# Twelve matmuls of a unit in another order: each weight part right behind the same stationary operand

## What is computed

```python
mod = silu(c) @ w_ada + b_ada                       # shift, scale, gate_res
h = rms(x) * norm_w * (1 + scale) + shift           # (256, 4096)
q, k, v, z_a, f_logit, x_r, z_r = split(h @ w_in)   # 4096 -> 12304 columns
y_a = (forgetting_attention(rms(q), rms(k), v, f_logit) * silu(z_a)) @ w_br_attn
y_r = (rg_lru(causal_conv(x_r)) * silu(z_r)) @ w_br_rnn
g_a, g_r = split(sigmoid(h @ w_gate + b_gate))
y = x + gate_res * ((g_a * y_a + g_r * y_r) @ w_out)
```

## Time and profile before

| | |
|---|---|
| time, median of 3 runs | 2731.93 us (2727.08 to 2733.43) |
| span of the profiled execution, first to last instruction | 2723.2 us |
| median less that span | 8.7 us |
| busy PE, PEld, DVE, ACT | 95%, 78%, 71%, 45% of the span |
| matmuls and weight loads | 11618 and 11618 |
| DMA | 701.95 MB, mean 258 GB/s |

### The profile page before, as it was taken

One profiled execution on the slowest core, in us unless ns is written; L12 is line 12 of the kernel. 1 busy time (PEld: TensorE's weight loads), 2 busy tenths in 40 slices (PEclk: granted clock), 3 DMA queues, 4 the chain that ended last, 5 costly groups with the idle time before them and its releaser, 6 DMA issues.

```text
span 2723.2 us, 37753 instructions
## 1 busy us (share of the span) xinstructions
PE 2580.2 (95%) x11618; PEld 2131.3 (78%) x11618; DVE 1929.6 (71%) x2038; ACT 1227.1 (45%) x1437; POOL 1.2 (0%) x9
## 2 busy tenths in 40 slices
PE   0199999999999999999999999999999999999999
PEld 0178888888888788787888888887888888788887
DVE  6688988989884656565666666668888888745454
ACT  1044444444445544445555555554444444433333
POOL 0000000000000000000000000000000000000000
PEclk9999999999999999999999999999999999999999
DMA  8999999999985565444666666669999999766665
GB/s 314 302 359 328 359 337 329 363 332 350 347 287 162 179 194 163 133 147 148 200 197 196 197 196 196 197 198 343 324 328 331 331 330 332 252 206 220 213 224 169
DMA packets 370084, 701.95 MB, mean 258 GB/s; under 512 B 26482, under 2 KB 30804, under 8 KB 369748
## 3 DMA queue, kind: packets, MB, share of 16 engines
q1 hardware_dynamic: 370004, 700.93, 76.6%
HBM read 696.65 MB, written 4.19 MB: 257 GB/s over the span
## 4 chain that ended last, share of the span: by engine, by line
PE 92%; DMA 3%; issue 2%; DVE 2%; ACT 1%; SPq 0%; ACTq 0%; DVEq 0%
PE ps_acc L1130 29%; PE ps_acc L1132 29%; PE ps_acc L1137 29%; DMA ada_land<-in_w_ada 2%; DVE acc L673 1%; DMA land<-in_w_gate 1%; PE ps_t L1229 1%; PE ps_t L1228 1%; PE ps_t L1293 1%; PE ps_c L1158 1%; ACT w_hi L451 0%; PE ps_t L1149 0%; PE ps_t L1286 0%; PE ps_c L1299 0%; PE ps_t L1220 0%
## 5 line engine op out<-in xcount | busy, mean ns | idle before, releaser
L659 DVE TENSOR_TENSOR w_lo<-land,w_hi 128x1024 fp32r<-128x1024 f32 x896 | 1093.8, 1222 | 622.1 <-ACT w_hi L451 618.8
L451 ACT ACTIVATE w_hi<-land 128x1024 fp32r<-128x1024 f32 x896 | 950.5, 1061 | 1253.2 <-PE ps_acc L1132 1090.6
L1130 PE MATMUL ps_acc<-w_hi,h_hi 128*128 128x512 f32 x3072 | 1207.3, 393 | 5.7 <-ACT w_hi L451 5.7
L1132 PE MATMUL ps_acc<-w_hi,h_lo 128*128 128x512 f32 x3072 | 1197.7, 390 | 0.0
L1137 PE MATMUL ps_acc<-w_lo,h_hi 128*128 128x512 f32 x3072 | 821.9, 389 | 3.7 <-DVE w_lo L659 3.7
L1130 PEld LDWEIGHTS ps_acc<-w_hi,h_hi 128*128 128x128 f32 x3072 | 577.7, 188 | 125.7 <-ACT w_hi L451 6.9
L1137 PEld LDWEIGHTS ps_acc<-w_lo,h_hi 128*128 128x128 f32 x3072 | 576.6, 188 | 124.9 <-DVE w_lo L659 4.1
L1132 PEld LDWEIGHTS ps_acc<-w_hi,h_lo 128*128 128x128 f32 x3072 | 577.9, 188 | 118.7
L673 DVE SCALAR_TENSOR_TENSOR acc<-ada_land,cvec,acc 128x1024 f32<-128x1024 f32 x248 | 317.1, 1279 | 32.0 <-DMA ada_land<-in_w_ada 28.1
L1008 DVE SCALAR_TENSOR_TENSOR racc<-res_land,cvec,racc 128x512 f32<-128x512 f32 x248 | 185.7, 749 | 4.9
L1130 PE MATMUL ps_acc<-w_hi,yr_hi 128*128 128x512 f32 x256 | 103.2, 403 | 0.0
(11 more groups left out here) (166 smaller groups left out, 1084.2 us busy)
## 6 DMA issues: line engine op xcount, KB each, us to landing
land<-in_w_in SPq DMA_DIRECT2D x384, 512.0 KB, 4.7
ada_land<-in_w_ada SPq DMA_DIRECT2D x256, 512.0 KB, 5.5
land<-in_w_gate SPq DMA_DIRECT2D x256, 512.0 KB, 4.3
res_land<-in_w_ada SPq DMA_DIRECT2D x128, 512.0 KB, 7.6
land<-in_w_out SPq DMA_DIRECT2D x128, 512.0 KB, 3.5
land<-in_w_br_attn SPq DMA_DIRECT2D x64, 512.0 KB, 3.5
land<-in_w_br_rnn SPq DMA_DIRECT2D x64, 512.0 KB, 5.8
gate<-in_b_gate SPq DMA_DIRECT2D x32, 256.0 KB, 5.2
```

What stands on the lines that cost most here:

```text
L451: act.activation(w_hi[:, u % PARTS], land[:, u % LAND], ACT.Copy).then_inc(hi_rdy, 1)
L659: dve.tensor_tensor(w_lo[:, u % PARTS], land[:, u % LAND], w_hi[:, u % PARTS].bitcast(F32), ALU.subtract).then_inc(split_done, 1)
L1130: pe.matmul(out, left_hi(kk, t), w_hi[:, u % PARTS, kk], start=first and kk == 0, stop=False)
L1132: ins = pe.matmul(out, left_lo(kk, t), w_hi[:, u % PARTS, kk], start=False, stop=False)
```

## The change

The twelve matmuls of `unit` are issued in another order, with (kk, t) after each: low left by high weights 00, high left by high weights 00, the same two for 01, then, after the wait for `split_done`, high left by low weights 01; low and high left by high weights 10, high left by low weights 10; low and high left by high weights 11, high left by low weights 11; and last high left by low weights 00. Three of the four matmuls by low weights so follow a matmul with the same stationary operand. The wait for the low weights stands before the fifth matmul and not before the ninth. `hi_used` is raised by the tenth matmul and not by the eighth, and `unit_done` by the twelfth as before. Nothing is added or left out.

```diff
-                for kk in range(UK):
-                    for t in range(NT):
-                        out = ps_acc[:, par, t]
-                        pe.matmul(out, left_hi(kk, t), w_hi[:, u % PARTS, kk], start=first and kk == 0,
-                                  stop=False)
-                        ins = pe.matmul(out, left_lo(kk, t), w_hi[:, u % PARTS, kk], start=False, stop=False)
-                ins.then_inc(hi_used, 1)
+
+                def by_hi(kk, t):
+                    out, right = ps_acc[:, par, t], w_hi[:, u % PARTS, kk]
+                    pe.matmul(out, left_lo(kk, t), right, start=first and kk == 0, stop=False)
+                    return pe.matmul(out, left_hi(kk, t), right, start=False, stop=False)
+
+                def by_lo(kk, t, end):
+                    return pe.matmul(ps_acc[:, par, t], left_hi(kk, t), w_lo[:, u % PARTS, kk],
+                                     start=False, stop=last and end)
+
+                by_hi(0, 0)
+                by_hi(0, 1)
                 pe.wait_ge(split_done, n0 + u + 1 + LAND)
-                for kk in range(UK):
-                    for t in range(NT):
-                        ins = pe.matmul(ps_acc[:, par, t], left_hi(kk, t), w_lo[:, u % PARTS, kk],
-                                        start=False, stop=last and kk == UK - 1)
-                ins.then_inc(unit_done, 1)
+                by_lo(0, 1, False)
+                by_hi(1, 0)
+                by_lo(1, 0, False)
+                by_hi(1, 1).then_inc(hi_used, 1)
+                by_lo(1, 1, True)
+                by_lo(0, 0, True).then_inc(unit_done, 1)
```

## The result

| | before | changed |
|---|---|---|
| median, 15 runs each | 2731.11 us | 2735.71 us |
| range | 2723.17 to 2734.51 us | 2734.54 to 2737.10 us |
| span of the profiled execution | 2723.2 us | 2734.4 us |

The ratio is 1.0022, with a 95% interval of 1.0014 to 1.0030. The two spans differ by 11.2 us, as the sum said (11). The two medians differ by only 4.6 us. Before's runs fall in two groups, 7 of 15 at or under 2727.1 us and 8 at or over 2731.1, and the changed kernel's in one.

A forecast was written before the change was run, and what follows sets the result against it. PE, carrying 92% of the chain, was taken as the bound. Stalls of 1.4 + 4.2 + 1.5 + 1.8 + 1.0 + 0.5 + 0.6 = 11 us on 2731.93 us gave 2743 us; range 2725 to 2750 us.

The forecast's parts named there:

- the distance of two starts: Between matmuls in a unit: stays 0.227 us despite repeated stationary operands and the new bank order; effect taken as 0.
- the rival: In the units' matmuls: a repeated stationary operand shortens the distance, gaining 7 to 27 us against 11 us of stalls; chance 0.18.
- The shift: In steady units: the later `hi_used` makes ACT's copy and DVE's subtraction 0.45 us later, reserve falling from 1.96 to 1.5 us.
- The stalls: Where low weights come too little ahead of the fifth matmul, PE waits: 11 us in sum, 5 to 20 us.
- Recurrent blocks: Units like 451 and 439: new stalls of 4.2 us and 1.5 us.
- unit 451's kind: In the recurrent blocks, once per 24 units: reserve 0.09 us, so 0.53 us of stall, 8 times, 4.2 us.
- unit 439's kind: In the recurrent blocks: reserve 0.40 us, so 0.22 us of stall, 7 times, 1.5 us.
- swallowed shift: At the tight places: PE's other products release DVE and ACT, so only unit 279 pays; 2733 us, chance 0.15.
- Squares and half-wave starts: Units 248 to 276, every fourth, behind ACT's squares: 0.22 us, 8 times, 1.8 us; six earlier half-wave starts: 1 us.
- Unit 279: Behind DVE's chain: 1.4 us more wait; a longer low-clock stretch, 0 to 1.6 us, taken as 0.
- The second merge pass: Unit 583 and four behind it: 0.5 us; waits for DVE in the last merge job: 0.6 us.
- 8.7 us around it: Time outside the profiled span, added to the 2734.2 us span to give 2742.9 us.

The follow-up runs named there:

- wait5: The kernel before with only the wait for the low weights moved from before the ninth to before the fifth matmul; median 2727.73 us, ratio interval 0.9978 to 0.9996.
- before_again: The kernel before, run once more with no edit; median 2732.75 us, ratio 0.9996 to the kernel before.
- spread_after: The changed kernel with the forget gate's 17 DVE scan operations issued two at a time behind units 286 to 303; median 2728.88 us, ratio 0.9994.
- best_after: The changed kernel with the forget gate's scan in pieces and z_r's sigmoid and product moved from unit 17 to 30; 2724.4 us, ratio 0.9983.
- best_before: The kernel before with the forget gate's scan in pieces and z_r's sigmoid and product moved from unit 17 to 30; 2715.9 us, ratio 0.9952.

## Why the prediction was right, step by step

**The bound, and the distance of two starts.** Both held. The distance did not move with the stationary operand, nor with the order of the banks: units 600 to 751 are the same to 0.01 us in all orders. The size of the rival was mis-added, though: 2743 less 7 to 27 us is 2716 to 2736 us with 2726 in the middle, not 2739 and 2724. The small product's 0.11 against 0.12 us did not carry over; the argument for that, that the load is shorter than the distance here and as long as it there, fits, but no run varied the load alone. Also by this the Trainium skill's sentence ("TensorE: Matmul & The Clock Gate", Part 2) that one can load once and multiply repeatedly finds nothing to save here: all 11618 loads are made in every order.

**The shift.** ACT's copy for unit 450 stood at 1466.85, 4.21 us before its unit's start (1473.78 - 2.72 = 1471.06); after the change at 1473.76, 3.75 us before (1480.23 - 2.72 = 1477.51). So it came 0.46 us later, 0.45 forecast.

**The stalls.**
- Recurrent blocks: 4.35 us of 5.7 forecast. The 8 places of unit 451's kind hold all of it, 4.35 / 8 = 0.54 us each, 0.53 forecast. The 7 of unit 439's kind cost nothing, and here the rival of a swallowed shift was right. In the changed kernel ACT waits for another product there:

```profile
1440.97 1.28 ACT L588 ACT_TABLE_LOAD   x1 [0.21 <-PE ps_t L1299]
...
1445.54 1.16 DVE L659 TENSOR_TENSOR w_lo<-land,w_hi 128x1024 fp32r<-128x1024 f32 x1
...
1447.09 0.39 PE L1134 MATMUL ps_acc<-w_lo,h_hi 128*128 128x512 f32 x1
```

  The chain to DVE begins at the product of line 1299, which the change doesn't move; the subtraction ends at 1446.70 and the reserve is 0.39 us, as before (0.40). The trace of before had it already, under that kernel's number for the same line, 1293:

```profile
1434.52 1.28 ACT L588 ACT_TABLE_LOAD   x1 [0.66 <-PE ps_t L1293]
```

  I had followed the chain back for unit 451 and taken it over to unit 439 unread.
- Squares and half-wave starts: by units, seven places behind the squares (248 to 276, without 256) cost 0.24 to 0.27 us each, 1.7 us together, where eight at 0.22 were forecast, 1.8. A half-wave is 40 units. The six starts (units 40, 80, 120, 160, 200 and 240) cost 0.2 to 0.3 us each, 1.6 together, forecast 1.0 as an estimate.
- Unit 279: 2.21 us, forecast 1.4. The waiting was longer by 5.03 - 3.68 = 1.35 us, as forecast; the rest is the low clock, whose stretch is longer and begins while matmuls of unit 279 are left. I had named this, 0 to 1.6 us, and taken 0. In the first trace of before the granted clock over 925 to 945 us is 0.91. It is 0.83 in the four traces with the early wait, here that of wait5, but also in before_again, the kernel before itself:

```profile
925.00:945.00 20.00, 15.42 (x56) 12.16 (x55) 13.64 (x22) 5.64 (x6) 0.00 (x0) 0.83 0.40 121
...
925.00:945.00 20.00, 16.32 (x60) 12.89 (x59) 13.16 (x22) 6.75 (x7) 0.00 (x0) 0.83 0.42 129
```

  That execution pays 1.23 us more here with nothing changed. So it isn't shown that the change makes the stretch longer, and about 0.8 of the 2.21 us may be chance.
- The second merge pass (units 576 to 767): 0.63 us in its first units and 0.89 in its last job, forecast 0.5 and 0.6. The first size says nothing, since five traces with both halves range from -0.21 to +0.71 there. The second is right in size for another reason than the one given: PE waits there for `h_lo`, not for low weights. The heads: 0, as taken.

The parts sum to 11.2 us over the spans, 11 forecast; that the errors of unit 439 (-1.5), unit 279 (+0.8) and the half-wave starts (+0.6) nearly cancel is luck.

**The absolute time** was off: 2743 us forecast, 2735.7 measured. The measured time lies below the forecast's own band, too (7 to 15 us of stalls over 2731.9, that is 2739 to 2747 us). By the times alone the swallowed shift (2733 us) was nearer, and the change is 4.6 us where 11 were forecast; only the stages decide for the forecast. The step that failed is the last line of the sum, "8.7 us around it", which takes the median less the span for what lies around the span. Around the span lie 1.8 us (2736.22 - 2734.4 for the profiled execution after, and within 0.1 of it in every run whose span is known), and 2734.2 + 1.8 = 2736.0 us. The other 7 us are the two groups: the profiled execution was of the lower one, the median of the upper one. The two ways to the forecast, from the span and from the median, are one sum only if both are of the same group. The granted clock of 0.999 and the range of 2727 to 2733 us over three runs were the only hints ahead. Of the difference of 4.6 us between medians the same holds: against the lower group of before (its 7 runs have a median of 2725.5 us) the change costs 10.2 us; over half of before's runs pay some 8 us for low-clock stretches that none of the changed kernel's 15 runs shows (by their times and clocks; one of them was traced). Why it hasn't them, although its stalls at units 337 and 369 are as long (1.56 and 1.52 us), stays open. It is not the order as such: spread_after, with the same order, had them in 2 of 12 runs. So half of the change's price in the medians is covered by an effect that no run here explains; best_after against best_before, without it, gives the price of the order itself.

## What to carry to other kernels

Operands that are made just ahead of use have a reserve, in us, at each place, and a change of order draws on it at both ends: what is needed earlier and what is released later add up, and stay free only until the sum passes the reserve of that place. Read the reserve at each kind of place, and follow the chain back to whatever releases it, since two places with the same rows in front can hang on different products. A repeated stationary operand is no gain where the loads are hidden and made anyway. And when one trace's span and the median of the runs lie further apart than a couple of us, look for two groups before you argue about tenths of a per cent.

## What the runs showed that I had not expected

A stall of PE of only 1.5 us can be followed by some 7 us at the lower clock in one execution and by none in another of the same kernel: 1.00 and 0.77 in the same 15 us stretch. Two such stretches make two groups of runs 8 us apart. And away from stalls a stage repeats to 0.01 us over 419 us, in all twelve traces here, so a comparison by stages shows what medians over 15 runs hide.
